# Moving operands of 512 columns in the ways down of five feed-forward layers, and an output projection on halves that are normalised afterwards

## What is computed

```
# the ways down: hidden is 2816 wide, each of the five layers ends with
x = x + 0.5 * ((silu(gate) * up) @ w_down)       # four times
x = x + gt2 * ((silu(gte) * val) @ w_down)       # once, in the last block

# the last block's mixer: attention and a gated convolution, 512 features each
mixed = concatenate([rmsnorm(attn, g_attn_out), rmsnorm(conv, g_conv_out)])
x = x + gt1 * (mixed @ w_out)
h = rmsnorm(x, g_ffn) * (1 + sc2) + sh2          # into the last feed-forward layer
```

## Time and profile before

| | us |
|---|---|
| median of 3 runs | 1866.95 |
| lowest and highest | 1866.34, 1868.29 |
| the profiled execution's own time | 1868.36 |
| its span | 1866.6 |
| PE busy in the span | 1764.6 (95%) |
| DVE busy | 1229.7 (66%) |
| ACT busy | 889.0 (48%) |
| POOL busy | 352.4 (19%) |

### The profile page before, as it was taken

One profiled execution on the slowest core, in us unless ns is written; L12 is line 12 of the kernel. 1 busy time (PEld: TensorE's weight loads), 2 busy tenths in 40 slices (PEclk: granted clock), 3 DMA queues, 4 the chain that ended last, 5 costly groups with the idle time before them and its releaser, 6 DMA issues.

```text
span 1866.6 us, 37048 instructions
## 1 busy us (share of the span) xinstructions
PE 1764.6 (95%) x16066; PEld 1675.2 (90%) x16066; DVE 1229.7 (66%) x2050; ACT 889.0 (48%) x1552; POOL 352.4 (19%) x308
## 2 busy tenths in 40 slices
PE   6999999999799999999999998979999999889997
PEld 6999978777699999999998877779999998779997
DVE  5876765655567785678675665556777565559974
ACT  5664434322345654566443432234565555346652
POOL 3562000000012561156100000001255200011110
PEclk9999999999799999999999999979999999889999
DMA  8655522101136655565552210113566553225442
GB/s 290 246 206 199 204 78 104 70 24 47 44 122 246 241 221 184 205 258 208 197 201 87 90 69 24 47 47 136 206 223 231 184 195 110 94 107 187 174 156 100
DMA packets 44498, 282.96 MB, mean 152 GB/s; under 512 B 6064, under 2 KB 6704, under 8 KB 17712
## 3 DMA queue, kind: packets, MB, share of 16 engines
q1 hardware_dynamic: 44336, 280.60, 41.3%
HBM read 279.53 MB, written 1.05 MB: 150 GB/s over the span
## 4 chain that ended last, share of the span: by engine, by line
PE 85%; DVE 8%; ACT 4%; issue 1%; DMA 1%; POOL 0%; SPq 0%; DVEq 0%; POOLq 0%; ACTq 0%
PE bank L485 20%; PE bank L487 20%; PE bank L486 20%; PE bank L971 10%; PE bank L1553 4%; DVE WL L476 2%; ACT WH L471 2%; PE bank L1820 1%; DMA ring<-wst 1%; PE bank L1111 1%; PE bank L516 1%; PE bank L1830 1%; DVE ML L1312 1%; PE bank L1843 1%; PE bank L673 0%
## 5 line engine op out<-in xcount | busy, mean ns | idle before, releaser
L485 PE MATMUL bank<-XNH,WH 128*128 128x256 f32 (+1 forms) x2176 | 621.4, 286 | 20.0 <-DVE XNL L562 12.6
L476 DVE TENSOR_TENSOR WL<-ring,WH 128x2048 fp32r<-128x2048 f32 (+1 forms) x235 | 509.9, 2171 | 180.1 <-ACT WH L471 179.7
L487 PE MATMUL bank<-XNH,WL 128*128 128x256 f32 (+1 forms) x2176 | 617.2, 284 | 0.0
L486 PE MATMUL bank<-XNL,WH 128*128 128x256 f32 (+1 forms) x2176 | 615.1, 283 | 0.0
L471 ACT ACTIVATE WH<-ring 128x2048 fp32r<-128x2048 f32 (+1 forms) x235 | 406.0, 1729 | 224.4 <-PE bank L487 174.5
L485 PEld LDWEIGHTS bank<-XNH,WH 128*128 128x128 f32 x2176 | 413.7, 190 | 25.6 <-DVE XNL L562 12.8
L486 PEld LDWEIGHTS bank<-XNL,WH 128*128 128x128 f32 x2176 | 415.2, 191 | 0.0
L487 PEld LDWEIGHTS bank<-XNH,WL 128*128 128x128 f32 x2176 | 414.9, 191 | 0.0
L485 PE MATMUL bank<-HH,WH 128*128 128x256 f32 x880 | 246.4, 280 | 0.7 <-POOL HL L868 0.6
L486 PE MATMUL bank<-HL,WH 128*128 128x256 f32 x880 | 246.2, 280 | 0.0
L487 PE MATMUL bank<-HH,WL 128*128 128x256 f32 x880 | 246.1, 280 | 0.0
(11 more groups left out here) (465 smaller groups left out, 2534.4 us busy)
## 6 DMA issues: line engine op xcount, KB each, us to landing
ring<-wst SPq DMA_DIRECT2D x206, 1024.0 KB, 4.8
ring<-wst SPq DMA_DIRECT2D x80, 704.0 KB, 4.1
LP<-lp SPq DMA_DIRECT2D x1, 1872.0 KB, 8.5
LP<-lp SPq DMA_DIRECT2D x1, 1792.0 KB, 8.7
X<-xin SPq DMA_DIRECT2D x2, 512.0 KB, 4.5
out<-X SPq DMA_DIRECT2D x4, 256.0 KB, 2.6
C<-cst SPq DMA_DIRECT2D x1, 193.0 KB, 10.7
AL<-cst SPq DMA_DIRECT2D x1, 192.0 KB, 10.8
```

What stands on the lines that cost most here:

```text
L476: e.do.tensor_tensor(WL[:, slot[q], 0:n], ring[:, i % NSLOT, 0:n], WH[:, slot[q], 0:n].bitcast(F32), ALU.subtract).then_inc(*w_dve.up("low ...
L485: e.do.matmul(o, WH[:, s, cols], xh, start=first, stop=False)
L486: e.do.matmul(o, WH[:, s, cols], xl, start=False, stop=False)
L487: return e.do.matmul(o, WL[:, s, cols], xh, start=False, stop=last)
```

## The change

It has two parts.

**Ways down.** HH and HL become one tensor HP with high and low part side by side for each hidden tile. For output tiles 0 to 6 the first two matmuls of a piece become one of 512 columns (`wide`): WH times high goes into columns 0 to 255 of the bank, WH times low into columns 256 to 511. WL times high follows with 256 columns, as before. DVE then adds both halves of the bank to x, one after the other, instead of one. Output tile 7 stays as it was.

**The last block's w_out.** The root of the norm is no longer multiplied into y. The high and low parts are of y times g (ACT with a scale, DVE and POOL), and can be made as soon as y is there. The products of attention's half go in columns 0 to 255, those of the convolution's half in columns 256 to 511 of the output tile's bank. ACT copies the spread root to SBUF (`roots`); DVE multiplies each half by it and then adds it, times gt1, to X2: four operations an output tile instead of one. In the order of turns, norm1 begins after six and not four steps of "first", PE's sums of norm0 come one turn later, "first" has two more steps, and DVE has a strand "first" of its own.

```diff
@@ second_order_of @@
-            return done["conv"] == steps["conv"] and done["first"] >= 4
+            return done["conv"] == steps["conv"] and done["first"] >= 6
...
+        def wide(e, b, q, cols, x, first, last):
+            s = slot[q]
+            e.do.matmul(b[:, :], WH[:, s, cols], x.rearrange("p s t -> p (s t)"), start=first, stop=False)
+            return e.do.matmul(b[:, 0:T], WL[:, s, cols], x[:, 0, :], start=False, stop=last)
...
@@ pe_ffn @@
-                        m = three(e, b[:, 0:T], q, slice(k * 128, k * 128 + 128), HH[:, kk, :], HL[:, kk, :], kk == 0, kk == NF - 1)
+                        at = slice(k * 128, k * 128 + 128)
+                        if n < KT - 1:
+                            m = wide(e, b, q, at, HP[:, kk, :, :], kk == 0, kk == NF - 1)
+                        else:
+                            m = three(e, b[:, 0:T], q, at, HH[:, kk, :], HL[:, kk, :], kk == 0, kk == NF - 1)
...
@@ dve_ffn @@
+                        xt, by = (X2[:, n, :], gt2[:, n:n + 1]) if f == 4 else (X[:, n, :], 0.5)
+                        if n < KT - 1:
+                            e.do.scalar_tensor_tensor(xt, bank[n][:, T:2 * T], by, xt, ALU.mult, ALU.add).then_inc(*f_dve.up())
+                            e.wait_ge(*f_dve.last())
+                        e.do.scalar_tensor_tensor(xt, bank[n][:, 0:T], by, xt, ALU.mult, ALU.add).then_inc(*f_dve.up("add", f, n))
...
+        def pe_out2_half(e, m, i):
+            q = turn_of("w_out_2", 0, ("two", m // 2))
             for n in range(4):
                 k = 4 * i + n
...
+                t = three(e, bank[m][:, T * i:T * i + T], q, slice(at, at + 128), yh, yl, n == 0, n == 3)
+            t.then_inc(*b_pe.up("out" if i else "out0", m))
...
         def pe_out2(e):
+            for m in range(2, KT):
+                if m < 6:
+                    e.wait_ge(*b_dve.on("taken", m))
+                else:
+                    e.wait_ge(*low_on(turn_of("w_out_2", 0, ("two", 3))))
+                    e.wait_ge(*n_act[m - 6].on("root"))
+                    pe_out2_half(e, m, 0)
+                pe_out2_half(e, m, 1)
+
+        def dve_out2_half(e, m, i):
+            q = scaled[:, i, :]
+            e.wait_ge(*n_act[i].on("root"))
+            e.wait_ge(*b_pe.on("out" if i or m >= 6 else "out0", m))
+            e.wait_ge(*b_dve.last())
+            e.do.tensor_tensor(q, bank[m][:, T * i:T * i + T], roots[:, T * i:T * i + T], ALU.mult).then_inc(
+                *(b_dve.up() if i else b_dve.up("taken", m)))
+            e.wait_ge(*b_dve.last())
+            e.do.scalar_tensor_tensor(X2[:, m, :], q, gt1[:, m:m + 1], X2[:, m, :], ALU.mult, ALU.add).then_inc(
+                *(b_dve.up("add", m) if i else b_dve.up()))
...
         def act_out2(e):
+            act_high(e, turn_of("w_out_2", 0, ("two", 3)))
...
         def dve_out2(e):
+            dve_low(e, turn_of("w_out_2", 0, ("two", 3)))
+            for m in (4, 5):
+                dve_out2_half(e, m, 0)
             for m in range(KT):
...
+                if m >= 6:
+                    dve_out2_half(e, m, 0)
+                dve_out2_half(e, m, 1)
+            dve_low(e, turn_of("w_out_2", 0, ("two", 1)) + AHEAD)
```

More of the change, by code:

```diff
@@ L624, in pe_ffn @@
                 elif f == 4:
-                    e.wait_ge(*b_dve.on("add", j + 6 if j < 2 else j))
+                    e.wait_ge(*b_dve.on("add", j))
                 for h in range(2):
@@ L2333, in act_norm2, with act_y2, act_y2_scaled @@
                 e.do.activation(norm_squares(i)[:, T * n:T * n + T], Y2[:, 4 * i + n, :], ACT.Square).then_inc(*n_act[i].up("sq"))
+            if i:
+                act_y2_scaled(e, i, gn)
             yield
+            if i == 0:
+                act_y2(e, i, gn)
+                act_y2_scaled(e, i, gn)
             yield
+            e.wait_ge(*n_pe[i].on("rows"))
+            e.do.activation(roots[:, T * i:T * i + T], bank[6 + i][:, 0:T], ACT.Copy).then_inc(*n_act[i].up("root"))
+            yield
+        def act_y2(e, i, gn):
             for n in range(4):
                 yh, yl = y2_parts(4 * i + n)
-                e.wait_ge(*n_dve[i].on("y", n))
-                e.do.activation(yh, Y2[:, 4 * i + n, :], ACT.Copy).then_inc(*n_act[i].up("yh", n))
-            yield
-        def y2_low(e, signal, i, n):
-            yh, yl = y2_parts(4 * i + n)
-            e.wait_ge(*n_act[i].on("yh", n))
-            e.do.tensor_tensor(yl, Y2[:, 4 * i + n, :], yh.bitcast(F32), ALU.subtract).then_inc(*signal.up("yl", n))
+                e.wait_ge(*(c_dve.on("y", n) if i else a_act[n].on("y", 1)))
+                e.do.activation(yh, Y2[:, 4 * i + n, :], ACT.Copy, scale=spc(gn, n)).then_inc(*n_act[i].up("yh", n))
+        def act_y2_scaled(e, i, gn):
+            e.wait_ge(*n_act[i].last())
+            for n in (0, 2):
+                e.do.activation(Y2[:, 4 * i + n, :], Y2[:, 4 * i + n, :], ACT.Copy, scale=spc(gn, n)).then_inc(*n_act[i].up("scaled", n))
         def dve_norm2(e, i, gn):
+            if i:
+                dve_y2(e, i, gn)
             yield
@@ L2486, in scalar_strands @@
             if l == DEPTH:
[L2487 removed]
+                return {"proj": act_project2(e), "norm0": act_norm2(e, 0, "gao"), "norm1": act_norm2(e, 1, "gco"),
                         **{f"att{j}": act_attend(e, j) for j in range(4)}}
@@ L2494, in vector_strands @@
                 return {"proj": dve_project2(e), "conv": dve_conv2(e), "norm0": dve_norm2(e, 0, "gao"), "norm1": dve_norm2(e, 1, "gco"),
+                        "first": dve_out2_first(e),
                         **{f"att{j}": dve_attend(e, j) for j in range(4)}}
```

82 lines of the change are left out of this document (40 added, 42 removed).

## The result

The changed kernel takes 1855.14 us (median of 4 runs, 1854.31 to 1855.83), the kernel before on the same chip 1866.64 (4 runs): a ratio of 0.9938 (0.9921 to 0.9955). That is 11.5 us faster where 25.7 were forecast, and above the range's upper end of 1850. The direction was right, the size was not.

A forecast was written before the change was run, and what follows sets the result against it. The prediction took PE, busy for 95% of the span, as the bound. Ways down 14.2 us plus last block 11.5 us gave 25.7 us off 1868.36, so 1842.7, as a median 1841 us; range 1834 to 1850.

The forecast's parts named there:

- A wide matmul streams for 213 ns: I take 216 for it: Ways down: 512 columns take 216 ns, 117 for the narrow one behind; 333 a pair against 352, 14.6 us over 770.
- only where load and stream are about as long: Ways down: a load shows as 10.6 ns at such lengths, and leaves 2.5 ns behind a stream of 213 ns.
- the load's share stays at every matmul: Rival, ways down: 10.6 ns come with every matmul whatever its length; ways down gain 7.8 us, total 1848; chance 0.20.
- rivals with 325 and with 544 ns for the pair: Ways down: both matmuls at columns plus 2.5 ns, total 1835 us (chance 0.10); 512 columns in two passes, 2003 (0.03).
- the walk: Last block: step-by-step times for each engine at PE's full clock, with the last layer starting 13.2 us earlier.
- With the hand-over 0.97 us: Last block's w_out on DVE: a half, multiplication plus addition, takes 0.97 us; twelve halves take 11.65 us.
- an addition (0.48): Last block's w_out on DVE: the addition in each half takes 0.48 us, beside a multiplication of 0.42.
- The fall of the clock: Last block: one fall of PE's clock after the new wait or around the sums costs 1.7 us, leaving 11.5 of 13.2.
- The new wait: Last block's w_out: PE waits 2.3 us for half 4, from 1629.4 to 1631.7.
- The end: Last block: low block of 2.29 us on DVE before the root, root at 1647.4, last layer 3.5 us later at 1650.9.
- new waits on DVE and ACT eat the second part: Rival, last block: halves take 1.2 us and the clock falls twice; part worth 6 us, total 1847; chance 0.12.
- the last layer's first matmul was to come 27 us earlier: Expected sign in the changed profile: 27 us or so earlier than 1664, 13 from the last block, 11.7 from four ways down.

The follow-up runs named there:

- e1: Separate small kernel of 64-matmul streams with no other engine at work; split type took 120.0, 173.4 and 227.3 ns for 256, 384 and 512 columns.
- e3: Changed kernel with three matmuls of 256 columns and one addition again in the ways down; 1858.69 us, 0.9956 of the kernel before.
- e2: Kernel before with only the ways down of the changed kernel; 1861.48 us, 0.9969 of the kernel before.
- e5: Changed kernel with the product written back to its PSUM bank for every second half and for tiles 6 and 7; 1850.69 us, ratio 0.9909.
- e6: Changed kernel with the first halves of tiles 4 and 5 ahead of the last low block on DVE; 1851.2 us, ratio 0.9909.
- e11: Changed kernel with products written back to PSUM, halves of tiles 4 and 5 ahead of the low block, and the old ways down; 1856.34 us, 0.9934.
- e4: Changed kernel with POOL's sums of squares in the last w_out cut from 256 to 8 columns; 1850.4 us, ratio 0.9915.
- e7: Changed kernel with products written back to PSUM and the halves of tiles 4 and 5 ahead of the low block; 1850.98 us, ratio 0.9908.
- e10: Repeat of e7 on the same chip as a rerun of the changed kernel; 1850.89 us, ratio 0.9914.

## Why the prediction was wrong

**Ways down, the term that was mis-sized: 14.2 us forecast, 4.0 by the five stages (5.5 by time, twice).** The step that failed is "A wide matmul streams for 213 ns: I take 216 for it": it measured 229.6 and the pair 347.1, not 333. The row it rested on, L971's 215.8 ns, is of another type: one of a plain float32 matmul's two records. The same argument had the addition show "only where load and stream are about as long"; e1 has 13 to 14 ns at 256, 384 and 512 columns alike. The rival "the load's share stays at every matmul" had the right shape, with 341.3 for the pair and 8.2 us, and half the owner: less load took 7 of the 13 ns off at 256 columns and nothing at 512, and bfloat16, with loads of as many columns, has only 2.5 ns. Even this bound was too good by 6 ns a pair, because 512 columns of the split type have 14 to 16 ns on top, 3 to 6 more than the 10.6 that the rows gave for 256. The rivals with 325 and with 544 ns for the pair fall. The extra additions on DVE were hidden, as said, and the last layer's way down gained 0.1 us less than the others by its wait for HP (0.4 forecast).

**The last block: 11.5 us forecast, 8.0 by the stretch, 8.2 by time (e3), 6.2 against e2's block.** Up to the sums of norm1 the walk held. It counts from the kernel before, where the block starts 4.8 us later (1506.8, now 1502.0), and its marks came 4.2 to 4.5 us ahead of the walk's times: bias of tile 23 at 1608.5 (walk 1612.9), end of w_out's first half 1616.0 (1620.2), of the convolution 1615.0 (1619.4), of the sums 1618.65 (1623.1). What failed lies behind that:
- "With the hand-over 0.97 us" for a half. Twelve halves took 15.05 us (1628.16 to 1643.21), not 11.65: 2.7 us by additions beside POOL (five times 0.5, and 0.15 and 0.06), 0.7 by a spacing of 1.04 us instead of 0.97 where nothing disturbs. This is the term. The step behind it is the price "an addition (0.48)", from the earlier trace rows: L2407 has one operand in PSUM, L2444 has two in SBUF. The trace of before had the answer under another name: L812 with operands FP and FA, both in SBUF, took 0.48 us in five cases and 0.96 in the seventeen in which a POOL operation (L868) had begun 0.16 us ahead of it (rows below), while L794, which reads PSUM, had a mean of 0.42 over its 88; 59 of these lay beside a POOL operation, and none took over 0.43. I had priced by operation and shape alone, and not by where the operands lie.
- The fall of the clock (window 1618.6 to 1622.1 at 0.51) cost about 1.5 of the 1.7 us that the forecast set for it: the 24 matmuls from 1618.65 on took 4.44 us, and in e5, which has no fall there, 2.93. (e5's sums ended 1.5 us later in the stretch, so that both stand at the same mark behind them; no gain of e5 is from this.) The second one (0.54, behind the new wait) hit PE while DVE ended the stage.
- The new wait was right in place, size (2.1 us, forecast 2.3) and cause: PE waited for half 4, which stands behind the low block on DVE. What the forecast didn't ask is whether it has to stand there; e6 took the wait away by letting that half go first.
- The end (low block in front of the root, 3.5 us from root to layer) came as walked: 1647.8 to 1651.3.

DVE and POOL of the kernel before, in order of time; L812 without and with POOL beside it:

```profile
1681.80 0.48 DVE L812 SCALAR_TENSOR_TENSOR FA<-FP,SP,FA 128x256 f32<-128x256 f32 x1
...
1687.51 0.96 DVE L812 SCALAR_TENSOR_TENSOR FA<-FP,SP,FA 128x256 f32<-128x256 f32 x1
```

```profile
1687.35 0.83 POOL L868 TENSOR_TENSOR HL<-HT,HH 128x256 fp32r<-128x256 f32 x1 [19.33 <-ACT HH L711]
```

The rival "new waits on DVE and ACT eat the second part" (6 us left, halves of 1.2 us) is the nearest to this part: 8.0 us left and 1.25 us for a half, 15.05 / 12. It named no reason for halves of 1.2 us, and had a chance of 0.12. The Trainium skill states the mechanism: SBUF — State Buffer, section Who interferes with whom, says that a DVE instruction with two SBUF inputs contends with a GpSimd instruction that reads SBUF, and one with at most one SBUF input, outside the 2-port perf modes, does not. The trace agrees (0.98 against 0.48, and 0.48 with the product in PSUM); with its 2.7 us the forecast for this part would have been 8.8.

Together: 10.2 us missing in the ways down by the stages, 3.5 in the last block; 25.7 less 13.7 is 12.0, and the measured ratio gives 11.5. The range failed because its slowest pair (341.3) was still taken from the addition at 256 columns, and because one chance of 0.12 carried every disturbance of DVE. Two of the prediction's signs don't fit its own walk: the last layer's first matmul was to come 27 us earlier, where its terms give 13.2 and 11.7, so 24.9 (it came 12.8 earlier); and there was to be no idle before tile 22, where the walk has 1.0 us (the trace 1.04).

## What to carry to other kernels

Price an operation by a row with the same type and the same places of its operands: a float32 row says nothing of the split type's pace, and an addition from PSUM nothing of one from SBUF beside a busy POOL. If DVE ends a stage while POOL works, let one of DVE's operands stay in PSUM; here a product written back over its bank gave 2.6 us for a changed line, and the order of three operations 2.0 more. Merging two matmuls into one of twice the columns saves at most the fixed part of one matmul, here 4.9 of 10.6 ns, so measure that part before counting on it. And compare the granted clock of a stretch before crediting its time to an edit: here unchanged code differed by 1.8 us.

## What the runs showed of the hardware

- Split-type matmuls (128 x 128 weights): 120.0, 173.4 and 227.3 ns for 256, 384 and 512 columns; bfloat16 109 and 216 for 256 and 512; plain float32 two records of 215.8 each for 256 columns and of 429 for 512. I had expected one pace for one array time.
- Alternating 512 and 256 columns costs 353.3 ns a pair in the bare stream, 6 more than the two kinds alone (227.3 and 120.0), and 347.1 in the kernel. Why is open.
- DVE's addition of two SBUF tensors: 0.48 us alone, 0.97 to 0.99 when a POOL sum of 0.74 us began 0.03 us before it, 0.54 when the sum had begun 0.46 us before; POOL's own time stayed at 0.72 to 0.74. Where DVE began first, POOL was the one that took longer: its low part L2396 took 2.71 us in the changed kernel when DVE's low block L476 (two SBUF inputs, 2.28 us) had begun 0.17 us before it, where before the same kind of part took 0.72:

```profile
1594.86 2.71 POOL L2396 TENSOR_TENSOR BIG2r<-Y,BIG2r 128x256 fp32r<-128x256 f32 x1 [97.11 <-ACT Y L2373]
```

- The same stretch of unchanged code, from the first to the second way down, took 493.0 and 492.0 us in the two profiled executions of the change, 492.1 in the kernel before, 490.6 to 492.2 in e2, e3, e6 and e11, and 489.2 in e4, e5, e7 and e10. The granted clock differs there: from 420 to 430 us it is 0.53 in the changed kernel's profile and 0.83 in e10's. So a single profiled execution tells stretches to some tenths where the granted clock agrees, and the whole only to a few us, and the gains of e4, e5 and e6 in time (4.7, 4.5 and 3.9 us below the change's median) are larger than in their stretch (2.5, 2.6 and 2.0). The profiled execution of e4, e5, e7 and e10 was in each case the shortest of its kernel, so the 489.2 may belong to these executions and not to the edits. The traces can't settle it.
